# Expert routing on one Trainium2 core: one operand of each large vector product placed in PSUM

## The reference, cut to what matters

```python
s = jnp.einsum('thcd,hcnd->thcn', q, sub_keys)
s1, i1 = lax.top_k(s[:, :, 0], K)
s2, i2 = lax.top_k(s[:, :, 1], K)
cand_s = (s1[..., :, None] + s2[..., None, :]).reshape(T, PEER_HEADS, K * K)
cand_i = (i1[..., :, None] * PEER_N_KEYS + i2[..., None, :]).reshape(T, PEER_HEADS, K * K)
top_s, top_pos = lax.top_k(cand_s, K)
expert_idx = jnp.take_along_axis(cand_i, top_pos, axis=-1)
gates = jax.nn.softmax(top_s, axis=-1)
```

## Time and profile before

| | us |
|---|---|
| median of 3 runs | 2817.05 (2815.21 to 2818.08) |
| profiled execution | 2817.18 |
| its span in the profile | 2815.4 |
| PE busy | 2691.1 (96%) |
| DVE busy | 1633.3 (58%) |
| ACT busy | 1400.3 (50%) |
| POOL busy | 595.9 (21%) |
| DMA, mean over the span | 159 GB/s |

### The profile page before, as it was taken

The page is one execution under the profiler, slowest core; times in us unless marked ns, Lnnn a source line. Parts: engine busy times, 40 slices in busy tenths (PEclk is TensorE's granted clock), DMA queues, the critical chain, the costliest instruction groups (busy, mean ns, idle before and its releaser), DMA issues.

```text
span 2815.4 us, 46276 instructions
## 1 busy us (share of the span) xinstructions
PE 2691.1 (96%) x16697; PEld 2371.4 (84%) x16714; DVE 1633.3 (58%) x2856; ACT 1400.3 (50%) x2305; POOL 595.9 (21%) x325
## 2 busy tenths in 40 slices
PE   8999999999999998799999999999999999989998
PEld 6689899998888875589899998888868977766896
DVE  3457936675555552357936675555555646554664
ACT  4334467764555443234467764445545445553543
POOL 0006976650000000006976650000000000000000
PEclk9899999999999999699999999999999999999999
DMA  6145454446555653045454446565555555434454
GB/s 208 60 147 169 157 169 137 142 143 199 191 192 191 193 169 95 35 143 169 158 167 136 143 143 198 194 193 192 191 168 174 186 180 163 141 93 150 144 185 149
DMA packets 124035, 447.60 MB, mean 159 GB/s; under 512 B 14280, under 2 KB 14920, under 8 KB 123648
## 3 DMA queue, kind: packets, MB, share of 16 engines
q1 hardware_dynamic: 119808, 434.16, 47.6%
q0 software_dynamic: 2608, 9.08, 1.1%
q10 hardware_dynamic: 1488, 2.59, 0.2%
HBM read 444.74 MB, written 1.05 MB: 158 GB/s over the span
## 4 chain that ended last, share of the span: by engine, by line
PE 83%; POOL 6%; DVE 5%; issue 3%; ACT 3%; DMA 0%; ACTq 0%; POOLq 0%; DVEq 0%
PE ps L708 40%; PE ps L680 11%; PE ps L686 11%; PE ps L683 11%; POOL w_lo L398 6%; PE ps L861 4%; DVE X L1521 1%; PE ps L658 1%; PE ps L917 1%; PE ps L740 1%; DVE big L1521 1%; PE ps L832 1%; PE ps L946 0%; DVE big L1514 0%; DVE x_lo L1568 0%
## 5 line engine op out<-in xcount | busy, mean ns | idle before, releaser
L386 ACT CAST w_hi<-ring 128x1024 fp32r<-128x1024 f32 (+1 forms) x808 | 846.0, 1047 | 1062.0 <-PE ps L708 571.1
L398 DVE TENSOR_TENSOR w_lo<-ring,w_hi 128x1024 fp32r<-128x1024 f32 (+1 forms) x640 | 782.1, 1223 | 833.6 <-ACT w_hi L386 824.4
L680 PE MATMUL ps<-x_hi,w_hi 128*128 128x256 f32 x3136 | 780.8, 287 | 3.5 <-DVE x_lo L1573 2.8
L683 PE MATMUL ps<-x_lo,w_hi 128*128 128x256 f32 x3136 | 768.3, 283 | 0.0
L680 PEld LDWEIGHTS ps<-x_hi,w_hi 128*128 128x128 f32 x3136 | 600.2, 191 | 7.2 <-issue 5.6
L683 PEld LDWEIGHTS ps<-x_lo,w_hi 128*128 128x128 f32 x3136 | 601.0, 192 | 0.0
L398 POOL TENSOR_TENSOR w_lo<-ring,w_hi 128x1024 fp32r<-128x1024 f32 x168 | 439.8, 2623 | 605.0 <-ACT w_hi L386 605.0
L686 PE MATMUL ps<-x_hi,w_lo 128*128 128x256 f32 x3136 | 442.1, 284 | 18.3 <-POOL w_lo L398 18.3
L708 PE MATMUL ps<-w_hi,x_hi 128*128 128x512 f32 x1488 | 412.9, 397 | 15.1 <-DVE x_lo L1568 10.9
L686 PEld LDWEIGHTS ps<-x_hi,w_lo 128*128 128x128 f32 x3136 | 404.1, 192 | 22.3 <-POOL w_lo L398 22.3
L708 PE MATMUL ps<-w_hi,x_lo 128*128 128x512 f32 x1488 | 406.2, 392 | 0.0
(11 more groups left out here) (232 smaller groups left out, 2055.9 us busy)
## 6 DMA issues: line engine op xcount, KB each, us to landing
ring<-in_u SPq DMA_DIRECT2D x256, 512.0 KB, 3.5
ring<-in_v SPq DMA_DIRECT2D x256, 512.0 KB, 4.0
ring<-in_ffn_in SPq DMA_DIRECT2D x88, 512.0 KB, 3.5
ring<-in_ffn_out SPq DMA_DIRECT2D x44, 512.0 KB, 3.5
ring<-in_wq SPq DMA_DIRECT2D x32, 512.0 KB, 3.5
ring<-in_ple_gate SPq DMA_DIRECT2D x16, 512.0 KB, 3.6
SC<-in_rows POOLq DMA_DIRECT2D x11, 512.0 KB, 4.8
ring<-in_a_qk SPq DMA_DIRECT2D x8, 512.0 KB, 4.4
```

Of the source, the lines that this page charges most:

```text
L386: nc.scalar.copy(part(w_hi, i)[:, used(name)], tile(i)[:, used(name)]).then_inc(tiles_hi, 1)
L398: eng.tensor_tensor(part(w_lo, i)[:, at], tile(i)[:, at], part(w_hi, i)[:, at], ALU.subtract).then_inc(tiles_low[LOW[n][0]], 1)
L680: mm = nc.tensor.matmul(bank(s)[:, 0:T], hi[:, k, :], x_hi[:, k, :], start=(k == 0), stop=False)
L683: nc.tensor.matmul(bank(s)[:, 0:T], hi[:, k, :], x_lo[:, k, :], start=False, stop=False)
```

## The change

Three operands move from SBUF to PSUM banks 0 to 2. `TIf`, the float indices, is written to bank 1 instead of in place in `tops`. `HL`, the float halves of positions, is written to bank 0 instead of `SC`. One copy is new: `firsts`, the values `TV`, in bank 2, from which the addition takes its first operand, the scores of the first list. The second operand of the addition is still `TV` in SBUF. The order and number of all other instructions stay.

```diff
-        TIf = shaped(tops[:, 512:1024], TB, 2 * H8, TOPK)
+        TIf = shaped(ps[:, 1, :], TB, 2 * H8, TOPK)
+        firsts = shaped(ps[:, 2, :], TB, 2 * H8, TOPK)
...
-        HL = shaped(SC[:, 2816:3328], 2, TB, H8, TOPK)
+        HL = shaped(ps[:, 0, :], 2, TB, H8, TOPK)
...
                 step(V.tensor_copy(TIf, TI))
-                wait()
-                v = lambda tb: TV[:, tb].rearrange("p (h c) k -> p h c k", c=2)
+                step(V.tensor_copy(firsts, TV))
+                wait()
+                v = lambda t, tb: t[:, tb].rearrange("p (h c) k -> p h c k", c=2)
                 c = shaped(SC[:, 0:2048], H8, TOPK, TOPK)
                 for tb in range(TB):
-                    tt(c, v(tb)[:, :, 0, :, None].to_broadcast([P, H8, TOPK, TOPK]),
-                       v(tb)[:, :, 1, None, :].to_broadcast([P, H8, TOPK, TOPK]), ALU.add)
+                    tt(c, v(firsts, tb)[:, :, 0, :, None].to_broadcast([P, H8, TOPK, TOPK]),
+                       v(TV, tb)[:, :, 1, None, :].to_broadcast([P, H8, TOPK, TOPK]), ALU.add)
```

## The result

The changed kernel takes **2790.18 us** (median of 4 runs, 2786.41 to 2791.61), against 2817.4 for the kernel before (4 runs). The ratio is 0.9903, with a 95% interval of 0.9891 to 0.9916: faster by about 1%. Forecast were 2793.9 us and a range of 2791.5 to 2798.5.

A forecast was written before the change was run, and what follows sets the result against it. PE was taken to bound the kernel, busy 96% of the span and losing 11.66 us per layer to late POOL tiles in the routing. 2 x 11.66 = 23.3 us off 2817.18 gave 2793.9, range 2791.5 to 2798.5.

The forecast's parts named there:

- PE's pace shows the loss, the waits don't: Routing tiles 0 to 49: 152.78 us against 141.12 at PE's own pace, a loss of 11.66 us per layer.
- the visible waits: PE's recorded waits for POOL at w_lo matmuls, 18.3 us in total; alone they would give 2798.9 us.
- Where the loss lies: Per layer in the routing: 9.76 us from four comparisons and four products, 1.90 from two additions.
- One input in PSUM leaves POOL alone, in both orders: In the routing, PSUM as first or second DVE input leaves POOL at 2.41 us per tile.
- two small operations with two SBUF inputs: Routing operations of 256 elements, 0.42 us each, holding POOL at most 0.42 us, within its 0.47 slack.
- DVE's times: In the routing: 2.28 us per large operation, 0.7 per 512-element write into PSUM, 0.42 per conversion of halves.
- the slower rival: DVE reads PSUM slowly in the routing's repeated, stepped pattern; at four times the plain time 2860 us, chance 0.02.
- The new wait and the cover: DVE's gates wait some 4 us for ACT's exponentials near tile 39; 30 us of DVE idle cover remain.
- The exponentials' block: ACT's table loads and exponentials near tile 40, taken to cost PE 0, at most 1.4 us per layer.
- The range: Whole kernel: 2791.5 to 2798.5 us, for run spread and pace rounding, upwards also the block at the exponentials.
- What a measurement can tell from no change: Whole-kernel time: about 0.2%, 5.6 us, can be told from no change.

The follow-up runs named there:

- compares_only: The changed kernel with only the float halves in PSUM, so of the large operations only the comparisons have one SBUF input; 2803.63 us, the kernel before there 2817.58.
- adds_only: The changed kernel with only the additions' first operand in PSUM, comparisons and products keeping two SBUF inputs; 2812.44 us, the kernel before there 2817.58.
- warm_after: The changed kernel plus 60 unread matmuls on zeros where PE idles before layer 1's attention; 2775.21 us, the kernel before there 2815.51.

## Why the prediction was right or wrong

- *PE's pace shows the loss, the waits don't.* Right: 141.12 us from tile 0 to 49. The gain in two routings is 23.3 and not the 18.3 of the visible waits, and the medians of the kernel pair with the added matmuls differ by 23.6.
- *Where the loss lies.* Right within 0.5 us per layer: 1.5 to 2.0 for the additions, where 1.90 was taken, and 9.7 to 10.2 for comparisons and products, where 9.76 was taken.
- *One input in PSUM leaves POOL alone, in both orders.* Right: POOL's tiles are at 2.41 us in the mean of the whole routing, and compares_only shows it for PSUM as the first input. The longest tile takes 2.61 us: it starts beside one of the two small operations with two SBUF inputs that the prediction listed, and stays within POOL's slack of 0.47.
- *DVE's times.* Right: 2.29 for the large operations, where 2.28 was taken, and 0.68 to 0.69 for the writes into PSUM, where 0.7 was taken. The two conversions of halves take 0.42 each, as taken. The Trainium skill, page "VectorE: DVE Perf Modes", section on the TRN2 errata, gives a source in PSUM a fixed cost that is 62 cycles higher than that of one in SBUF. This is not seen here: 2286 and 2291 ns with an input in PSUM against 2284 in the earlier trace rows. Nor does the slow pattern of the slower rival appear.
- *The new wait and the cover.* Right: 4.73 us for ACT, 30.77 us left. The exponentials' block cost PE nothing: no wait is left in the stretch.
- *The range.* Wrong, and this step failed: "for the spread of the three runs (about 1.5 us)". With it the sum put everything outside the two routings at no change, without a term for it. The time of this kernel moves by 9 us from run to run: 42 runs of the kernel before lie between 2811.9 and 2820.73. Its trace had shown a granted clock of 0.979 over the span, and the stretch at the lower level stood in it; the prediction used the clock only of the routing's windows, where it is 1.00. The missing term is the attention's stretch, which the profiled execution of before had at 259.9 us and the others without added matmuls at 251.7 to 263.2. Put in after the fact, it turns 2793.9 into a range of 2785.7 to 2797.2, which holds both medians, 2790.18 and 2793.84. That the second falls on the forecast is as much chance as that the first missed the range.
- *What a measurement can tell from no change.* The prediction had 0.2%, which was about right: the intervals here reach 0.10 to 0.21% to either side. With 10 and 13 runs even adds_only, whose routing is 2.0 us shorter per layer, came out at 0.9986 with an interval of 0.9976 to 0.9996.

## What to carry to other kernels

When GpSimd works beside the vector engine on SBUF data, count the vector operations with two SBUF inputs. In this kernel each took turns with GpSimd, and one input in an unused PSUM bank freed both engines at the price of a plain copy, or of none where the operand could be written there in the first place. Look also for short vector operations with one SBUF input that take 2 us or more beside GpSimd; here they were hidden. Measure what such a stall costs by the pace of the bound engine, from tile to tile, and not by its recorded waits. And look at the granted clock in every stretch ahead of a prediction, since a stretch at the lower level may make the whole time vary by more than the edit is worth; matmuls on zeros in the idle time ahead of it gave 17 to 19 us in the medians here, and 13 to 14 in the means, since in some runs they did not help.

## What was not expected of the hardware

The clock fell in an idle time of PE of 6.2 us and stayed at its lower level for some 20 to some 40 us in the same code, while the stretch took from 251.7 to 263.2 us. In warm_after, with that idle time and the one of 7.1 us before it filled, the stretch took 243.8 us. The best kernel of the study is that one, 2775.21 us, 1.3% under the kernel before, of which the change to the routing is 23.3 us. The traces do not show why a conversion or shift with a single SBUF input was held and a sum was not.
